# Last norm's second part: the spread of the factors by rounded single passes in place of native fp32 matmuls

## The chip, the cores and the metric

The kernel runs on one core of one Trainium2 chip. The metric is the device time of one execution in microseconds (us); the median of several executions counts. Engines run their own instruction streams and wait for each other by semaphores: TensorE (matmuls; PE in the rows, its weight loads PEld), VectorE (DVE), ScalarE (ACT), GpSimd (POOL) and SyncE (SP, which issues most DMAs here).

## What is computed

One layer of an encoder on x of 1024 tokens by 1024 channels: a SwiGLU block, a gated mixer, a cross-attention, a second SwiGLU block, and a last RMS norm. Only this last norm is touched:

```python
def _rms_norm(v, g):
    vf = v.astype(jnp.float32)
    r = lax.rsqrt(jnp.mean(vf * vf, axis=-1, keepdims=True) + EPS)
    return (vf * r).astype(v.dtype) * g

h = h + 0.5 * _swiglu(_rms_norm(h, ffn2_norm[l]), ffn2_w_gate[l], ffn2_w_up[l], ffn2_w_down[l])
return _rms_norm(h, final_norm)
```

## The kernel before

Activations lie transposed in SBUF: `h` has 8 tiles m of 128 channels (on the partitions) by 1024 tokens. Token columns are treated in two halves of 512, c = 0 and c = 1. Nearly all of the kernel is matmuls at line 550, each fp32 operand split in a high and a low half of the rounded type fp32r (`x_hi`, `x_lo`), three single-pass products for one of full precision. A matmul of native fp32 leaves two weight loads and two passes in the trace, one of fp32r leaves one of each.

The down projection of the second SwiGLU finishes the half c = 1 of `h` first, then the half c = 0. The last norm therefore comes in two parts, first for c = 1, beside the last matmuls, then for c = 0, when no other matmul is left. The steps of a part:

- ScalarE squares tiles of `h`, VectorE adds the squares into `acc`, and TensorE sums over the channels with one-column matmuls against `ones` (`last_sums`, lines 789 and 796). The sums come out as columns: 128 tokens on the partitions, one column for each of the 4 blocks of 128 tokens.
- VectorE forms the mean (`mean_square`, line 1943), ScalarE the square root (`root`), VectorE the reciprocal and one correction step (`factor_columns`, lines 1968 to 1978). The factors then stand in `norm[:, 2, 0:4]`.
- The factors must be spread: each of the 128 partitions needs the factor of every token along its row. This is `last_spread`. For c = 1 the factors are split in halves, `norm_hi` (a cast to fp32r) and the rest, each is multiplied with the identity into `diag_hi`, `diag_lo` (128x512), and `ones_r` times these gives the rows: two passes of 512 columns, beside other matmuls. For c = 0 the column of factors, broadcast along the free axis to 128x128, is the stationary operand and `ident` the moving one, native fp32, for 4 blocks of tokens into each of two PSUM banks (lines 803 to 807): first `last_bank(0, 1)`, which VectorE reads, then `last_bank(1, 0)`, which ScalarE copies to `f_g` for GpSimd. A semaphore `s_fsp` is raised after each bank. TensorE waits for `s_fac` at 4 before it.
- VectorE multiplies its tiles by the gain and the factor (`scale_last`, line 2479: six tiles for c = 0), and GpSimd two (tiles 5 and 7), which ScalarE has multiplied by the gain beforehand. SyncE stores each tile of VectorE's as it is done (line 1186), ScalarE's queue stores those of GpSimd (line 1395). Each store is 128 partitions by 512 columns, 256 KB, eight for each half.

The order of the end is written out by hand: VectorE scales tiles 1 to 3 of c = 1 around the mean of c = 0, adds the last sum (line 2462), waits for ScalarE's root, does `factor_columns(n, s_fac)` (line 2463), and goes to the six scalings. At the start of the kernel (from line 2023) VectorE casts `ones` to `ones_r`, and does four small operations, before it waits for TensorE.

Of the kernel before, what the change touches and what calls it, by code (L numbers as in the profile page):

```python
# [5 lines left out]
F32 = mybir.dt.float32  # L6
F32R = mybir.dt.float32r
ALU = mybir.AluOpType
# [3 lines left out]
P = 128  # L12
# [3 lines left out]
HALF = 512  # L16
# [227 lines left out]
def build(nc, a):  # L244
    ctx = ExitStack()
    with ctx:
        def sem(name):
            return ctx.enter_context(nc.semaphore(name))

        def tensors(where, specs):  # L250
            return [where.enter_context(nc.sbuf_tensor(n, s, d)) for n, s, d in specs]
# [4 lines left out]
        with ExitStack() as v:  # L256
            diag_hi, diag_lo = tensors(v, [("diag_hi", [P, L], F32R), ("diag_lo", [P, L], F32R)])
        sq, rn = tensors(ctx, [("sq", [P, L], F32), ("rn", [P, L], F32)])
        gains, ones, ident = tensors(ctx, [("gains", [P, 6, KT], F32), ("ones", [P, P], F32), ("ident", [P, P], F32)])
        ones_r, norm_hi, nidx, turn8 = tensors(ctx, [("ones_r", [P, P], F32R), ("norm_hi", [P, L // P], F32R),  # L260
                                                     ("nidx", [P, NC], F32), ("turn8", [P, COLS], F32)])
        pscale, m8, dskip, edge, eye = tensors(ctx, [
# [2 lines left out]
        stat, norm, mem_rows = tensors(ctx, [("stat", [P, 2, 4, 4], F32), ("norm", [P, 4, L // P], F32),  # L265
                                             ("mem_rows", [P, N_MEM // P], F32)])
# [59 lines left out]
        def scratch(name, shape, dt=F32):  # L326
# [26 lines left out]
        s_msq, s_total, s_fac, s_fsp, s_mg, s_mn, s_xn = (sem(n) for n in  # L353
            ("mem_squared", "squares_totalled", "norm_on_diagonals", "first_norm_spread", "mem_scaled", "mem_normed",
             "x_normed"))
# [92 lines left out]
        def ffn_bank(f, *use):  # L448
            r = BANK_AT[f][use] % 8
            pair = (finished["pairs", f] + f + r // 2) % 4  # L450
            return ps[pair if f else FIRST_PAIRS[pair]][:, r % 2]
# [68 lines left out]
        def key_bank(j):  # L520
            return (ps[3][:, 0], ps[3][:, 1], ps[2][:, 0], ps[2][:, 1])[j]

        def last_bank(c, k):

            return ffn_bank(1, "dn", 5, 2 * (1 - c) + k)
# [17 lines left out]
        def _(pe):  # L543
# [256 lines left out]
            def last_spread(c):  # L800
                pe.wait_ge(s_fac, 4 - c)
                if c == 0:
                    for bank in (last_bank(0, 1), last_bank(1, 0)):
                        for t in range(HALF // P):
                            ins = nc.tensor.matmul(bank[:, t * P:(t + 1) * P], norm[:, 2, t:t + 1].to_broadcast([P, P]),
                                                   ident[:], start=True, stop=True)
                        ins.then_inc(s_fsp, 1)
                    return
                nc.tensor.matmul(last_bank(c, 1), ones_r[:], diag_hi[:, 0:HALF], start=True, stop=False)
                nc.tensor.matmul(last_bank(c, 1), ones_r[:], diag_lo[:, 0:HALF], start=False, stop=True).then_inc(s_fsp, 1)  # L810
# [52 lines left out]
            for k in range(KT):  # L863
                w = kv_weights(k)
                pe.wait_ge(s_mg, k + 1)
                for t in range(2):
                    for c in range(2):
                        ins = nc.tensor.matmul(ps[t][:, c], mem_g[:, k, t * P:(t + 1) * P],  # L868
                                               w[:, c * HALF:(c + 1) * HALF], start=k == 0, stop=k == KT - 1)
# [17 lines left out]
            for m in range(KT):  # L887
# [5 lines left out]
                for k in range(KT):  # L893
                    ins = nc.tensor.matmul(key_bank(m // 2)[:, (m % 2) * N_MEM:(m % 2 + 1) * N_MEM], w[:, k],  # L894
                                           mem_n[:, k], start=k == 0, stop=k == KT - 1)
# [164 lines left out]
            ffn(1)  # L1060
            last_sums(0)
            last_spread(0)
            assert next(passes, None) is None

# [842 lines left out]
        def _(dve):  # L1907
# [3 lines left out]
            v = nc.vector  # L1911

            def link(ins, tally=step):

                tally.add()
                ins.then_inc(tally.sem, 1)
                dve.wait_ge(tally.sem, tally.at())

            def wait_act():
                dve.wait_ge(s_a2d, from_act.add())  # L1920
# [15 lines left out]
            def tt(out, x, y, op=ALU.mult, tally=step):  # L1936
                link(v.tensor_tensor(out, x, y, op), tally)  # L1937

            def ts(out, x, s1, s2=None, op0=ALU.mult, op1=None, tally=step):
                if op1 is None:  # L1940
                    link(v.tensor_scalar(out, x, s1, None, op0), tally)
                else:
                    link(v.tensor_scalar(out, x, s1, s2, op0, op1), tally)
# [4 lines left out]
            def cp(out, x, tally=step):  # L1948
                link(v.tensor_copy(out, x), tally)
# [18 lines left out]
            def factor_columns(n, signal=None, tally=step):  # L1968

                x, root, y, z = (norm[:, k, 0:n] for k in range(4))  # L1970
                wait_act()
                link(v.reciprocal(y, root))
                tt(z, y, y)
                tt(z, z, x)
                ts(z, z, -0.5, 1.5, ALU.mult, ALU.add)
                if signal:
                    v.tensor_tensor(y, y, z, ALU.mult).then_inc(signal, 1)
                else:
                    tt(y, y, z, tally=tally)
                return y, z  # L1980
# [41 lines left out]
                tt(mem_sq[:, 0:n], mem_sq[:, 0:n], mem_sq[:, n:2 * n], ALU.add, tally=totals if n == 1 else step)  # L2022
            dve.wait_ge(s_const, 16 * 2)
            cp(ones_r[:], ones[:])
            q = PL
            dve.wait_ge(s_pl, 16)
            tt(q["t4"], q["ar"], q["ar"])
# [13 lines left out]
            n = L // P  # L2041
# [4 lines left out]
            y, z = factor_columns(n, tally=to_act)  # L2046
# [161 lines left out]
            def ffn(f, gi, new=None, behind=lambda n: None, next_lo=None):  # L2208
# [167 lines left out]
                for n in range(f, FT):  # L2376
# [7 lines left out]
                    if f and n == 1:  # L2384
                        dve.wait_ge(s_spread, 1)
                        for c in range(2):
                            ins = v.tensor_copy(rn[:, c * HALF:(c + 1) * HALF], ffn_bank(f, "spread", c))
# [63 lines left out]
                if f == 0:  # L2451
                    next_low(f, KT - 1, KT - 2, next_lo, gi + 1)
                    for q in range(MP, KT):
                        add_next(f, q)
                else:
                    n = HALF // P
                    scale_last(1, 1)
                    scale_last(2, 1)
                    mean_square(last_bank(0, 0), n, step)
                    scale_last(3, 1)  # L2460
                    dve.wait_ge(s_norm, norms.add())
                    stt(norm[:, 0, 0:n], last_bank(1, 0)[:, 0:n], 1.0 / D, norm[:, 0, 0:n], ALU.mult, ALU.add, tally=to_act)
                    factor_columns(n, s_fac)
                    for m in range(KT):
                        if m not in POOL_FIRST:
                            scale_last(m, 0)
# [71 lines left out]
            def next_low(f, q, m, dst_lo, gi):  # L2538

                if m >= KT - 2:  # L2540
                    by, count = dn_op(f, DN_N - 2 if m == KT - 1 else DN_N - 3).low
                    dve.wait_ge(s_w_low[by], count)
                dve.wait_ge(s_bhi, q + 1)
                stt(dst_lo[:, m], h[:, m], gains[:, gi, m:m + 1], ua_hi[:, m].bitcast(F32), ALU.mult, ALU.subtract, tally=to_pe)
# [329 lines left out]
```

## Time and profile before

| | us |
|---|---|
| median of 3 runs | 2038.44 |
| lowest, highest | 2038.42, 2039.1 |
| the profiled execution | 2039.92 |
| its span, first to last instruction | 2038.1 |

| engine | busy us | share |
|---|---|---|
| TensorE | 2017.5 | 99% |
| VectorE | 1411.9 | 69% |
| GpSimd | 1199.4 | 59% |
| ScalarE | 654.5 | 32% |

The rows come from the one profiled execution. Times in them are us from the start of the span; PEclk is the clock that was granted to TensorE as a share of 2.4 GHz. A share of busy time is a mean over stages with different limits; here only the last 16 us and a few of the first are concerned, and they are read by timelines and by tables of short windows.

### The profile page before, as it was taken

What the parts mean: (1) busy time and instruction counts of PE and PEld (TensorE: products, weight loads), DVE (VectorE), ACT (ScalarE), POOL (GpSimd) and SP (SyncE); (2) the same over time, 40 slices, a digit from 0 to 9 for tenths busy, and PEclk for the clock granted to TensorE, in tenths of its full rate; (3) what the DMA queues carried; (4) which work ended last, traced back from release to release, by engine and by line L of the source; (5) the groups of instructions that cost most, each with busy time, mean ns of one, the idle gap of its engine ahead of it and who ended that gap; (6) DMA issues with size and microseconds to landing.
All of it is one profiled execution on the core that took longest, in us unless ns stands there. A gap on an engine that the chain in (4) does not pass through costs nothing.

```text
span 2038.1 us, 24606 instructions
## 1 busy us (share of the span) xinstructions
PE 2017.5 (99%) x9222; PEld 1657.4 (81%) x9222; DVE 1411.9 (69%) x1609; ACT 654.5 (32%) x1002; POOL 1199.4 (59%) x803
## 2 busy tenths in 40 slices
PE   9999999999999999999999999999999999999997
PEld 5888888888888888888888888787788888888886
DVE  7788768756976978663252455447876876789687
ACT  6423322333444501002131223235323233244443
POOL 6498888886545533223324321236899989865453
PEclk9999999999999999999999999999999999999999
DMA  7524333447976472432113331301233232288663
GB/s 272 177 79 152 105 138 104 144 161 283 311 236 218 128 189 69 124 95 56 52 50 126 106 122 45 122 32 62 79 134 98 85 128 99 88 295 289 221 211 135
DMA packets 141078, 286.39 MB, mean 141 GB/s; under 512 B 12832, under 2 KB 38048, under 8 KB 140576
## 3 DMA queue, kind: packets, MB, share of 16 engines
q1 hardware_dynamic: 100528, 232.68, 33.9%
q10 hardware_dynamic: 40432, 52.13, 8.0%
q8 instruction: 74, 1.21, 0.2%
q14 instruction: 44, 0.36, 0.1%
HBM read 222.39 MB, written 63.42 MB: 140 GB/s over the span
## 4 chain that ended last, share of the span: by engine, by line
PE 90%; DVE 6%; ACT 1%; issue 1%; POOL 1%; DMA 0%; POOLq 0%; SPq 0%; DVEq 0%; ACTq 0%
PE ps L550 86%; PE ps L894 1%; PE ps L868 1%; DVE w_lo L2527 1%; DVE h L2536 1%; DVE xt_lo L2517 1%; DVE ua_lo L1946 0%; DVE acc L1937 0%; POOL w_lo L1202 0%; DVE f_g L1937 0%; ACT xb_hi L1494 0%; DMA raw<-in_kv 0%; POOL h L1375 0%; POOL raw L1227 0%; ACT prob L1384 0%
## 5 line engine op out<-in xcount | busy, mean ns | idle before, releaser
L1202 POOL TENSOR_TENSOR w_lo<-raw,w_hi 128x512 fp32r<-128x512 f32 x352 | 543.2, 1556 | 197.4 <-ACT w_hi L1446 196.6
L550 PE MATMUL ps<-xt_hi,w_hi 128*128 128x512 f32 x1320 | 514.9, 390 | 2.7 <-DVE xt_lo L2517 1.4
L550 PE MATMUL ps<-xt_hi,w_lo 128*128 128x512 f32 x1320 | 513.6, 389 | 0.0
L550 PE MATMUL ps<-xt_lo,w_hi 128*128 128x512 f32 x1320 | 513.6, 389 | 0.0
L1446 ACT ACTIVATE w_hi<-raw 128x512 fp32r<-128x512 f32 x462 | 284.6, 625 | 460.7 <-PE ps L550 316.5
L1217 POOL TENSOR_SCALAR w_hi<-raw 128x1024 fp32r<-128x1024 f32 x53 | 62.4, 1178 | 456.5 <-PE ps L550 386.2
L550 PEld LDWEIGHTS ps<-xt_hi,w_hi 128*128 128x128 f32 x1320 | 247.7, 188 | 56.7 <-issue 2.5
L550 PEld LDWEIGHTS ps<-xt_hi,w_lo 128*128 128x128 f32 x1320 | 247.8, 188 | 51.8
L550 PEld LDWEIGHTS ps<-xt_lo,w_hi 128*128 128x128 f32 x1320 | 247.8, 188 | 50.9
L1227 POOL TENSOR_TENSOR raw<-raw 128x512 f32<-128x512 f32 x177 | 263.6, 1500 | 16.4 <-DMA raw<-in_gu 9.1
L550 PE MATMUL ps<-ua_hi,w_hi 128*128 128x512 f32 x608 | 237.4, 390 | 0.1
L550 PE MATMUL ps<-ua_lo,w_hi 128*128 128x512 f32 x608 | 236.6, 389 | 0.0
L1282 POOL TENSOR_TENSOR raw<-raw 128x512 f32<-128x512 f32 x110 | 164.7, 1502 | 121.1 <-DMA raw<-in_dn 120.7
L550 PE MATMUL ps<-xb_hi,w_hi 128*128 128x512 f32 x528 | 206.9, 392 | 2.2 <-POOL w_lo L1202 1.6
L550 PE MATMUL ps<-xb_lo,w_hi 128*128 128x512 f32 x528 | 205.6, 389 | 0.0
L550 PE MATMUL ps<-xb_hi,w_lo 128*128 128x512 f32 x528 | 205.5, 389 | 0.0
L550 PE MATMUL ps<-ua_hi,w_lo 128*128 128x512 f32 x608 | 187.3, 389 | 0.0
L1219 POOL TENSOR_TENSOR w_lo<-raw,w_hi 128x1024 fp32r<-128x1024 f32 x53 | 142.6, 2690 | 4.4
L2325 DVE TENSOR_TENSOR f_g<-ps,f_g 128x512 f32<-128x512 f32 x156 | 107.7, 690 | 45.1 <-ACT f_g L1548 21.0
L550 PEld LDWEIGHTS ps<-ua_hi,w_hi 128*128 128x128 f32 x608 | 114.1, 188 | 24.9 <-issue 0.9
L550 PEld LDWEIGHTS ps<-ua_hi,w_lo 128*128 128x128 f32 x608 | 114.1, 188 | 23.9
L550 PEld LDWEIGHTS ps<-ua_lo,w_hi 128*128 128x128 f32 x608 | 114.2, 188 | 23.5
(324 smaller groups left out, 2857.6 us busy)
## 6 DMA issues: line engine op xcount, KB each, us to landing
raw<-in_dn SPq DMA_DIRECT2D x264, 256.0 KB, 3.4
raw<-in_gu SPq DMA_DIRECT2D x88, 512.0 KB, 5.0
raw<-in_weights SPq DMA_DIRECT2D x54, 512.0 KB, 3.5
d_act<-f_g SPq DMA_DIRECT2D x20, 512.0 KB, 2.8
d_act<-acc SPq DMA_DIRECT2D x20, 512.0 KB, 2.8
d_act<-sq SPq DMA_DIRECT2D x20, 512.0 KB, 4.2
xt_hi<-d_act SPq DMA_DIRECT2D x20, 512.0 KB, 5.4
xt_lo<-d_act SPq DMA_DIRECT2D x20, 512.0 KB, 4.9
```

The costliest lines, as they stand in the source:

```text
L550: ins = nc.tensor.matmul(out, lhsT, rhs, start=start, stop=stop)
L868: ins = nc.tensor.matmul(ps[t][:, c], mem_g[:, k, t * P:(t + 1) * P], w[:, c * HALF:(c + 1) * HALF], start=k == 0, stop=k == KT - 1)
L894: ins = nc.tensor.matmul(key_bank(m // 2)[:, (m % 2) * N_MEM:(m % 2 + 1) * N_MEM], w[:, k], mem_n[:, k], start=k == 0, stop=k == KT - 1)
L1202: add(lo, src, hi.bitcast(F32), op=ALU.subtract).then_inc(s_w_low["pool"], 1)
L1217: nc.gpsimd.tensor_scalar(hi, src, 1.0, 0.0, ALU.mult, ALU.add).then_inc(s_w_hi, 1)
L1219: add(lo, src, hi.bitcast(F32), op=ALU.subtract).then_inc(s_w_low["pool"], 1)
L1227: add(out, x, y, op=op).then_inc(s_w_sum, 1)
L1282: add(raw_part(op, 0), raw_part(op, 0), raw_part(op, 1), op=ALU.add if w[2] > 0 else ALU.subtract).then_inc(s_w_sum, 1)
L1446: nc.scalar.activation(w_hi[:, op.halves[0]].rearrange("p k c -> p (k c)"), src, ACT.Copy).then_inc(s_w_high, 1)
L2325: link(v.tensor_tensor(out, x, y, ALU.add), adds)
L2517: v.tensor_tensor(xt_lo[:, 3, d % 4], acts_at(d // FP, d % FP), xt_hi[:, 3, d % 4].bitcast(F32), ALU.subtract).then_inc(s_a_lo, 1)
L2527: v.tensor_tensor(lo, raw_part(op, 0), hi.bitcast(F32), ALU.subtract).then_inc(s_w_low["dve"], 1)
```

## The change

For the half c = 0 the factors are now split in halves as well: `norm_hi` by a cast and a new tile `norm_lo` by a subtraction on VectorE, and the signal `s_fac` comes with the latter. `last_spread` makes two accumulating matmuls a block in place of one, with the broadcast column of `norm_hi` and then of `norm_lo` as the stationary operand and `ident_r`, a new fp32r copy of the identity, as the moving one. `ident_r` is cast once at the start, behind `ones_r`.

```diff
--- before.py
+++ after.py
@@ -257,6 +257,7 @@
             diag_hi, diag_lo = tensors(v, [("diag_hi", [P, L], F32R), ("diag_lo", [P, L], F32R)])
         sq, rn = tensors(ctx, [("sq", [P, L], F32), ("rn", [P, L], F32)])
         gains, ones, ident = tensors(ctx, [("gains", [P, 6, KT], F32), ("ones", [P, P], F32), ("ident", [P, P], F32)])
+        ident_r, norm_lo = tensors(ctx, [("ident_r", [P, P], F32R), ("norm_lo", [P, HALF // P], F32R)])
         ones_r, norm_hi, nidx, turn8 = tensors(ctx, [("ones_r", [P, P], F32R), ("norm_hi", [P, L // P], F32R),
                                                      ("nidx", [P, NC], F32), ("turn8", [P, COLS], F32)])
         pscale, m8, dskip, edge, eye = tensors(ctx, [
@@ -802,8 +803,9 @@
                 if c == 0:
                     for bank in (last_bank(0, 1), last_bank(1, 0)):
                         for t in range(HALF // P):
-                            ins = nc.tensor.matmul(bank[:, t * P:(t + 1) * P], norm[:, 2, t:t + 1].to_broadcast([P, P]),
-                                                   ident[:], start=True, stop=True)
+                            for part in (norm_hi, norm_lo):
+                                ins = nc.tensor.matmul(bank[:, t * P:(t + 1) * P], part[:, t:t + 1].to_broadcast([P, P]),
+                                                       ident_r[:], start=part is norm_hi, stop=part is norm_lo)
                         ins.then_inc(s_fsp, 1)
                     return
                 nc.tensor.matmul(last_bank(c, 1), ones_r[:], diag_hi[:, 0:HALF], start=True, stop=False)
@@ -2022,6 +2024,7 @@
                 tt(mem_sq[:, 0:n], mem_sq[:, 0:n], mem_sq[:, n:2 * n], ALU.add, tally=totals if n == 1 else step)
             dve.wait_ge(s_const, 16 * 2)
             cp(ones_r[:], ones[:])
+            cp(ident_r[:], ident[:])
             q = PL
             dve.wait_ge(s_pl, 16)
             tt(q["t4"], q["ar"], q["ar"])
@@ -2460,7 +2463,9 @@
                     scale_last(3, 1)
                     dve.wait_ge(s_norm, norms.add())
                     stt(norm[:, 0, 0:n], last_bank(1, 0)[:, 0:n], 1.0 / D, norm[:, 0, 0:n], ALU.mult, ALU.add, tally=to_act)
-                    factor_columns(n, s_fac)
+                    y, _ = factor_columns(n)
+                    cp(norm_hi[:, 0:n], y)
+                    v.tensor_tensor(norm_lo[:], y, norm_hi[:, 0:n].bitcast(F32), ALU.subtract).then_inc(s_fac, 1)
                     for m in range(KT):
                         if m not in POOL_FIRST:
                             scale_last(m, 0)
```

## Rows read from the trace of the kernel before

**Rows 1.** The page: busy us, share of the span and instructions of each engine.

```profile
PE 2017.5 (99%) x9222; PEld 1657.4 (81%) x9222; DVE 1411.9 (69%) x1609; ACT 654.5 (32%) x1002; POOL 1199.4 (59%) x803
```

**Rows 2.** Timeline of TensorE from 2022.9 us: start, length, instruction, releaser.

```profile
2023.14 0.95 PE L789 MATMUL ps<-ones,acc 128*128 128x1 f32 x8
2024.87 1.16 PE L796 MATMUL ps<-ones,sq 128*128 128x1 f32 x8 [0.79 <-ACT sq L1642]
2027.98 3.78 PE L805 MATMUL ps<-ident,norm 128*128 128x128 f32 x16 [1.94 <-DVE norm L1977]
```

**Rows 3.** Timeline of VectorE, the last six scalings.

```profile
2030.09 4.04 DVE L2479 SCALAR_TENSOR_TENSOR h<-h,gains,ps 128x512 f32<-128x512 f32 x6 [2.17 <-PE ps L805]
```

**Rows 4.** Timelines of ScalarE, GpSimd and ScalarE's queue, last 8 us.

```profile
2031.80 0.60 ACT L1626 ACTIVATE f_g<-ps 128x512 f32<-128x512 f32 x1 [5.04 <-PE ps L805]
2032.47 2.49 POOL L1375 TENSOR_TENSOR h<-h,f_g 128x512 f32<-128x512 f32 x2 [5.16 <-ACT f_g L1626]
2033.77 1.58 ACTq L1395 DMA_DIRECT2D out<-h  x2
```

**Rows 5.** Table of windows: busy time by engine, granted clock, DMA share, GB/s.

```profile
core 0: us, PE busy (x) PEld busy (x) DVE busy (x) ACT busy (x) POOL busy (x), PEclk, DMA share, GB/s
2025.00:2025.60 0.60, 0.60 (x7) 0.60 (x7) 0.60 (x2) 0.00 (x0) 0.60 (x1) 1.00 0.00 0
2025.75:2030.75 5.00, 3.06 (x15) 2.97 (x15) 2.36 (x8) 0.21 (x1) 1.56 (x2) 0.50 0.98 365
2030.75:2031.75 1.00, 1.00 (x5) 0.71 (x4) 1.00 (x3) 0.00 (x0) 0.00 (x0) 0.50 0.08 27
2031.75:2037.25 5.50, 0.01 (x1) 0.00 (x0) 2.38 (x4) 0.60 (x1) 2.49 (x2) 0.81 1.01 379
```

**Rows 6.** DMA issues from 2022 us: count, KB each, us from issue to landing.

```profile
out<-h SPq DMA_DIRECT2D x14, 256.0 KB, 2.1
out<-h ACTq DMA_DIRECT2D x2, 256.0 KB, 2.7
```

**Rows 7.** Timeline of VectorE in the norm's first part.

```profile
2015.84 0.17 DVE L1937 TENSOR_TENSOR norm<-norm 128x4 f32<-128x4 f32 x1
2016.04 0.17 DVE L1949 CAST norm_hi<-norm 128x4 fp32r<-128x4 f32 x1
...
2016.45 0.69 DVE L1937 TENSOR_TENSOR diag_hi<-ident,norm_hi 128x512 fp32r<-128x512 f32 x1
```

**Rows 8.** Timeline of TensorE in a narrow window (2028.6 to 2029) of the spread.

```profile
2028.35 1.06 PE L805 MATMUL ps<-ident,norm 128*128 128x128 f32 x4
```

**Rows 9.** Timeline of TensorE in the attention: rounded passes, then native ones.

```profile
1197.34 0.28 PE L550 MATMUL ps<-k_hi,ua_hi 128*128 128x256 f32 x1
1197.46 0.28 PE L550 MATMUL ps<-k_lo,ua_hi 128*128 128x256 f32 x1
...
1212.56 0.93 PE L1009 MATMUL ps<-ident,prob 128*128 128x128 f32 x7
```

**Rows 10.** Weight loads by line and shape: count, busy us, mean ns.

```profile
L550 PEld LDWEIGHTS ps<-xt_hi,w_hi 128*128 128x128 f32 x1320 | 247.7, 188 | 56.7 <-issue 2.5 <-DVE acc L2325 1.5 <-DVE xt_lo L2237 1.0
...
L550 PEld LDWEIGHTS ps<-u_t,e_m 128*64 128x64 f32 x128 | 6.9, 136 | 1.2 <-issue 0.4
...
L789 PEld LDWEIGHTS ps<-ones,acc 128*128 128x128 f32 x16 | 2.1, 191 | 0.2
...
L833 PEld LDWEIGHTS ps<-tables 128*32 128x32 f32 x64 | 1.5, 109 | 1.4 <-issue 0.7 <-DVE f_g L2325 0.7
```

**Rows 11.** Line 805: weight loads, ns min/median/max; then a narrow window with the first two.

```profile
L805 PEld LDWEIGHTS ps<-ident,norm x16: 285/333/333, 2028.0 to 2031.1; 128*128 128x128 f32 x16
...
2027.98 0.50 PEld L805 LDWEIGHTS ps<-ident,norm 128*128 128x128 f32 x2 [2.03 <-DVE norm L1977]
```

**Rows 12.** Timeline of VectorE at the start of the kernel.

```profile
11.09 0.23 DVE L1949 CAST ones_r<-ones 128x128 fp32r<-128x128 f32 x1
...
13.78 0.16 DVE L1943 TENSOR_SCALAR norm<-ps 128x2 f32<-128x2 f32 x1 [1.55 <-PE ps L851]
```

## The prediction

> **What bounds the kernel now.** Over the whole span it is TensorE, busy 99% [rows 1]. The change, though, touches only the last 10 us, so I read that stretch by itself: first the timeline of each engine, then the table by short windows, then the DMA issues. What TensorE does from 2022.9 us on [rows 2] is: eight one-column passes (the sums of squares), a wait, eight more, a wait of 1.94 us for VectorE's `norm`, and then the spread at line 805: 16 records in 3.78 us, with nothing else left beside them. Its 8 calls are native fp32, and each leaves two records of 128 columns. VectorE [rows 3] starts its six scalings at 2030.09, when the first bank (8 of the 16 records) is done; ScalarE starts the copy for GpSimd at 2031.80, when all 16 are [rows 4]. So the spread is on the path: nothing of it is hidden by TensorE's own work.
>
> Behind it comes a second limit. In the table of windows [rows 5] the DMA engines are full (0.98 at 365 GB/s) until 2030.75 with the stores of the half c = 1, then all but idle for the next 1.00 us (0.08), and full again (1.01 at 379 GB/s) for the 5.50 us to 2037.25. Eight stores of 256 KB [rows 6] are 2.10 MB, and at 379 GB/s these take 5.5 us: that is the whole of the last stretch. The end of the kernel is therefore the start of the first store of the half c = 0, plus 5.5 us of full DMA engines, plus 0.9 us to the end of the span. That first store follows VectorE's first scaling, so the **first bank** sets the end by this way; the **second bank** sets it another way (ScalarE's copy 0.60, two GpSimd products 2.49 to 2034.96, two stores issued from ScalarE's queue), and there the last store takes 2.7 us to land against 2.1 for one that finds the engines free [rows 4, 6]. So that way has 0.5 to 0.6 us to spare. And a gain has a ceiling: the idle time of the DMA engines is about 0.9 us (1.00 x 0.92), and stores that come earlier than that only queue behind those of the half c = 1.
>
> **The change part by part.** (1) VectorE: behind the last multiply of the factors it gains a cast to `norm_hi` and a subtraction to `norm_lo`, both 128x4, and the signal to TensorE moves behind the second. The same two operations stand in the first part of the same norm [rows 7]: multiply at 2015.84, cast at 2016.04, then the subtraction, and what follows it at 2016.45. So they cost 2016.45 - 2015.84 less the 0.20 of the multiply alone: **+0.41 us**, in full on the path, since TensorE waits for exactly this. Queued behind them on VectorE are only the six scalings, which wait for TensorE anyway. TensorE's first load moves from 2027.98 to about 2028.39.
>
> (2) TensorE: 8 calls of two records become 16 calls of one record, so 16 weight loads and 16 passes of 128 columns stay 16 and 16. What can shrink is the time of one. Before, records follow at 213 ns: the rows of narrow windows give 1.06 us for 4 of 421 ns each, (1.06 - 0.42) / 3 [rows 8]. That is 256 cycles at 1.2 GHz for 128 columns, two cycles for each; the granted clock there is 0.50 of 2.4 GHz, where it was 1.00 up to 2025.6, and fell after the one-column passes and the wait between them [rows 5]. A pass of the rounded type (fp32r) needs one cycle for a column: passes of 256 columns follow at 0.12 us at the full clock (1197.34, 1197.46), as long as native fp32 takes for half the columns there ((0.93 - 0.27) / 6 = 0.11 for 128) [rows 9]. If only the streaming counted, a 128-column pass would now cost 107 ns.
>
> But every pass has its own weight load, and the load doesn't get cheaper. Its cost is seen where nothing is streamed: the eight one-column passes at the full clock take 0.95 us [rows 2], the last of them 250 ns long, so (0.95 - 0.25) / 7 = 0.10 us apiece. The recorded load times give the same in another way: 109 ns for 32 columns, 136 for 64, 191 for 128 [rows 10], 0.85 ns a column, two cycles of 2.4 GHz, so about 107 ns for 128. And fp32r loads are no shorter than native ones: 188 ns for `w_hi` against 191 for native `ones` [rows 10]. At the clock of the spread the load record is 333 ns instead of 191 [rows 10, 11], longer by 142; a doubled 107 accounts for 107 of it, and a doubled 53 would account for 53. So I take the load as 256 cycles: 213 ns at 1.2 GHz, just what the native pass took. Loads run ahead under passes, so the spacing is the longer of the two: max(213, 107) = 213 ns, and the stream of 16 is as long as before. Two corrections remain. The last pass of each bank streams 107 ns less behind its load: -0.1 us. The fp32r passes show some 12 ns on top of their streaming (0.12 against 0.107) [rows 9]: +0.1 us for 8, +0.2 for 16. Together **-0.1 to +0.1 us**, taken as 0.
>
> (3) `cp(ident_r, ident)`, a cast of 128x128, at the start. The same cast of `ones` took 0.23 us [rows 12]. Soon behind it VectorE waits 1.55 us for TensorE's first sums: hidden, 0 us; were that cover gone it would cost 0.26. The spread needs its result 2 ms later. (4) Two more tensors (512 and 16 bytes a partition) move what is allocated behind them. No row prices that; the repeats of one program lie within 0.7 us, and I take 0, with 0.3 either way.
>
> **Sum**, against the profiled execution (span 2038.1, its own time 2039.92): +0.41 + 0 + 0 = +0.4. First bank 0.4 later, first store 0.4 later, the DMA engines full for the same 5.5 us; second bank 0.4 later and inside its spare 0.5 or with it. Span 2038.5. The median of the runs, 2038.44, is 1.5 below the profiled one; from it, **2038.8 us**, and 2038.4 to 2039.3 with the bounds above. If the clock were high during the spread, both kinds would follow at about 0.11 us [rows 2, 9] and the sum would be the same.
>
> **Rivals.** *Cheap passes* (faster): the fp32r load takes one cycle a column after all, or overlaps better, and passes follow at 107 ns. First bank: 7 intervals shorter by 106 and the last pass by 107, -0.85, with the 0.41 a net -0.4: the DMA stream starts 0.4 earlier and the time is 2038.0. The second bank gains 15 x 0.106 + 0.1 - 0.41 = 1.3, of which nothing arrives, since its stores find the engines full. It breaks even at a spacing of 213 - (0.41 - 0.11)/7 = 170 ns. With a clock that is high as well it goes to the ceiling of 0.9: 2037.5. For it speaks the unexplained rest of the load record (142 against 107) and that the second load of the spread starts only 0.17 us after the first (0.50 - 0.333) [rows 11]; against it the slope of the load times. 0.16. [...]
>
> *Dear short passes* (slower): an fp32r pass narrower than 256 columns doesn't reach one cycle a column but four, or is split. The narrowest fp32r passes of the trace are those of 256 columns [rows 9], so nothing excludes it. Then 427 ns each at 1.2 GHz. First bank: 7 x 0.214 + 0.21 + 0.41 = +2.1; the stream of stores starts 2.1 later: 2040.6. If the clock stays low to the end of it, the second bank decides: 15 x 0.214 + 0.21 + 0.41 = +3.8, less the 0.6 that its way has to spare: 2041.6. It decides from 213 ns upwards for every ns; 0.2% of the time (4.1 us, about what a measurement of this kernel can tell from no change) would need some 490 ns a pass. Against it speaks only that 256 columns show no penalty. 0.17.
>
> *Something in the placement or the rest* that moves the 2000 us before, either way: 0.05.
>
> **How the numbers follow.** Forecast as likeliest 0.62: 2038.8. To hold 8 in 10 the range must take in most of both rivals: 2037.6 to 2041.6. No case but the last reaches 0.2% (2034.4 or 2042.5): faster 0.01, same 0.96, slower 0.03.
>
> **What would show it.** After: line 805's records single, 16 or so, at 213 ns and each about 314 ns long instead of 421; the first one at about 0.4 us further from `norm`; VectorE's scalings and ScalarE's copy both 0.3 to 0.5 later against the last sums; the DMA gap 0.4 longer and the full stretch again 5.5 us. A spacing near 107 ns at clock 0.50 proves the first rival and the load term wrong, one near 427 the second. Stores of the half c = 0 that do not start with VectorE's first scaling would prove the DMA part wrong.

## The result

| | before | after |
|---|---|---|
| median of the runs, us | 2038.44 | 2087.65 |
| lowest, highest | 2038.42, 2039.1 | 2087.34, 2087.87 |
| the profiled execution, its span | 2039.92, 2038.1 | 2087.54, 2085.7 |

The changed kernel takes 1.0239 times as long, 95% interval 1.0227 to 1.0252: 49 us more, where 2038.8 us was predicted. Those 49 us cannot lie in the last norm: the part of it that the change touches lasted 10 us before. The page of after shows the engines as before [rows 1], with the same 9222 passes, and 50 us more of busy TensorE; then the chain of waits, and three groups of the costliest ones (busy us, mean ns of one, idle before):

```profile
span 2085.7 us, 24609 instructions
PE 2067.2 (99%) x9222; PEld 1655.3 (79%) x9222; DVE 1396.9 (67%) x1612; ACT 655.2 (31%) x1002; POOL 1184.1 (57%) x803
...
PE 94%; DVE 2%; ACT 1%; DMA 1%; POOL 1%; issue 1%; POOLq 0%; SPq 0%; DVEq 0%; ACTq 0%
...
L551 PE MATMUL ps<-xt_hi,w_hi 128*128 128x512 f32 x1320 | 522.1, 396 | 0.9 <-POOL w_lo L1204 0.5
L551 PE MATMUL ps<-xt_lo,w_hi 128*128 128x512 f32 x1320 | 521.4, 395 | 0.0
```

The same two views of before, the chain and one of the groups:

```profile
PE 90%; DVE 6%; ACT 1%; issue 1%; POOL 1%; DMA 0%; POOLq 0%; SPq 0%; DVEq 0%; ACTq 0%
...
L550 PE MATMUL ps<-xt_hi,w_hi 128*128 128x512 f32 x1320 | 514.9, 390 | 2.7 <-DVE xt_lo L2517 1.4
```

TensorE was the bound and is it still more: its share of the chain went from 90% to 94%, VectorE's fell from 6% to 2%. And line 551, the old line 550, which the change does not touch, has longer records: 396 ns against 390. Records of passes overlap, so the price of one pass is read from starts. TensorE in the middle of the kernel, before, three starts of the same step:

```profile
639.64 0.39 PE L550 MATMUL ps<-xt_hi,w_hi 128*128 128x512 f32 x1
...
640.32 0.39 PE L550 MATMUL ps<-xt_hi,w_hi 128*128 128x512 f32 x1
...
641.00 0.39 PE L550 MATMUL ps<-xt_hi,w_hi 128*128 128x512 f32 x1
```

and after:

```profile
640.04 0.39 PE L551 MATMUL ps<-xt_hi,w_hi 128*128 128x512 f32 x1
640.27 0.40 PE L551 MATMUL ps<-xt_lo,w_hi 128*128 128x512 f32 x1
640.50 0.39 PE L551 MATMUL ps<-xt_hi,w_lo 128*128 128x512 f32 x1
640.74 0.40 PE L551 MATMUL ps<-xt_hi,w_hi 128*128 128x512 f32 x1
```

A step of three passes took 0.68 us and takes 0.70. As a mean over the 1250 or so unbroken steps of `xt` in a trace it is 680.2 ns before and 700.1 after, 226.7 and 233.4 a pass. A window of 34 us in which TensorE is never idle counts the same thing (passes that overlap its ends are counted in): first before, then after. The granted clock is 1.00 in both, so this is no clock.

```profile
core 0: us, PE busy (x) PEld busy (x) DVE busy (x) ACT busy (x) POOL busy (x), PEclk, DMA share, GB/s
640.00:674.00 34.00, 34.00 (x152) 28.15 (x151) 27.80 (x37) 17.30 (x29) 19.88 (x13) 1.00 0.59 184
```

```profile
640.00:674.00 34.00, 34.00 (x147) 27.30 (x146) 24.95 (x35) 13.96 (x24) 20.32 (x15) 1.00 0.65 211
```

The kernel makes 8136 such passes, three-pass products with a weight of `w_hi` or `w_lo` and 512 columns streamed: 3 x 1320 of `xt`, 3 x 608 of `ua`, 3 x 528 of `xb`, 3 x 128 of `ub`, and 192 each of `mixed` and `y`. The mean start-to-start (of starts less than 300 ns apart) of every one of these six kinds rose from between 226.7 and 227.1 to 233.2 or 233.3 ns. 8136 x 6.5 ns = 53 us, of which 49 reach the end. Some 2 us of the rest went into waits that TensorE had before (its idle time fell from 20.6 to 18.5 us): with slower passes VectorE is late less often, which is its fall in the chain. The other 2 are not placed: the product counts every pass as part of an unbroken stream, and not all are.

Nor is it traffic of the other engines. Among the `xt`, `ua` and `xb` passes there are 372 after during which VectorE, ScalarE and GpSimd were idle and no DMA packet was under way: their mean is 233.3 ns. The 326 such passes before have 226.8.

What the change does to these passes is only to move one of their operands. In SBUF `w_hi` and `w_lo` are allocated ahead of `ident_r` and `norm_lo`, the streamed operands behind. In the program built from the kernel before, `w_hi` starts at byte 16512 of a partition and `xt_hi` at 130176; in that of after, at 16512 and at 130720, 544 bytes later. Of the 544, `ident_r` has 512, from 62784, and `norm_lo` 32 for its 16, from 63296 to `ones_r` at 63328. The runs count in the same way: the change with 32, 96 or 224 more unused bytes goes like the kernel before with a plain pad of 64, 128 or 256 (steps of 686.7, 700.0 and 680.2 ns, both times), so its own tensors count as 544, and not as 528.

### The profile page after: what moved, and what is told of

The parts are those of the page before. It is cut to its first block, busy times and chain, and to the rows that moved or that the text cites. A ratio compares the mean times of both kernels' runs of the same rounds, so it can differ in the third digit from the quotient of the medians.

```text
span 2085.7 us, 24609 instructions
## 1 busy us (share of the span) xinstructions
PE 2067.2 (99%) x9222; PEld 1655.3 (79%) x9222; DVE 1396.9 (67%) x1612; ACT 655.2 (31%) x1002; POOL 1184.1 (57%) x803
## 4 chain that ended last, share of the span: by engine, by line
PE 94%; DVE 2%; ACT 1%; DMA 1%; POOL 1%; issue 1%; POOLq 0%; SPq 0%; DVEq 0%; ACTq 0%
PE ps L551 91%; PE ps L896 1%; DMA raw<-in_kv 1%; PE ps L870 1%; POOL w_lo L1204 0%; DVE f_g L1939 0%; ACT xb_hi L1496 0%; POOL h L1377 0%; POOL raw L1229 0%; ACT prob L1386 0%; DVE ua_lo L1939 0%; ACT ua_hi L1386 0%; DVE stat L2737 0%; DVE pt_lo L1939 0%; PE ps L823 0%
## 5 line engine op out<-in xcount | busy, mean ns | idle before, releaser
L1204 POOL TENSOR_TENSOR w_lo<-raw,w_hi 128x512 fp32r<-128x512 f32 x352 | 531.5, 1520 | 236.5 <-ACT w_hi L1448 235.2
L551 PE MATMUL ps<-xt_hi,w_hi 128*128 128x512 f32 x1320 | 522.1, 396 | 0.9 <-POOL w_lo L1204 0.5
L551 PE MATMUL ps<-xt_lo,w_hi 128*128 128x512 f32 x1320 | 521.4, 395 | 0.0
L551 PE MATMUL ps<-xt_hi,w_lo 128*128 128x512 f32 x1320 | 521.4, 395 | 0.0
L551 PE MATMUL ps<-ua_lo,w_hi 128*128 128x512 f32 x608 | 240.9, 396 | 0.0
```

What stands on the lines that cost most here:

```text
L551: ins = nc.tensor.matmul(out, lhsT, rhs, start=start, stop=stop)
L1204: add(lo, src, hi.bitcast(F32), op=ALU.subtract).then_inc(s_w_low["pool"], 1)
```

## The experiments

Two numbers are given for each run: the median with its ratio to before on the same chip, and the **step**, the mean of a step of three `xt` passes in its trace. "Distance" is by how many bytes the start of the streamed operands was moved against that of the weights, against before; there all these starts lie multiples of 1024 bytes apart. The expectations name the rule that I held when each was written: first the placement against the instructions of the change, then a start that must be a multiple of 64 bytes, then a distance by 128, and at last one by 256. Ratios in brackets are 95% intervals.

### Is it the change or the place?

The kernel before with two tensors that nobody uses, of the size of the new ones:

```diff
+        tensors(ctx, [("pad_a", [P, 128], F32)])
+        tensors(ctx, [("pad_b", [P, 4], F32)])
```

> The kernel before with nothing changed but two unused tensors of 512 and 16 bytes a partition, allocated where the change puts ident_r and norm_lo (544 bytes with the rounding to 32). In the changed kernel all passes of 512 columns with w_hi or w_lo as weights follow at 233.3 ns instead of 226.7. Theory A (placement: what is allocated behind the two tensors starts 32 bytes past a multiple of 64 instead of on one, and the passes read slower there): 2087.3, as the changed kernel, with 233.3 ns. Theory B (the new instructions do it, in whatever way): 2038.4 with 226.7 ns.

2087.72 us, ratio 1.024 (1.0226 to 1.0254), step 700.1 ns: the whole loss, without one instruction of the change. Its passes:

```profile
640.00 0.39 PE L552 MATMUL ps<-xt_lo,w_hi 128*128 128x512 f32 x1
640.23 0.40 PE L552 MATMUL ps<-xt_hi,w_lo 128*128 128x512 f32 x1
640.47 0.39 PE L552 MATMUL ps<-xt_hi,w_hi 128*128 128x512 f32 x1
640.70 0.40 PE L552 MATMUL ps<-xt_lo,w_hi 128*128 128x512 f32 x1
```

The change with its two tensors allocated behind `h`, so that no operand of the long products moves:

```diff
         gains, ones, ident = tensors(...)
-        ident_r, norm_lo = tensors(...)
...
         h = ...
+        ident_r, norm_lo = tensors(...)
```

> The change with all its instructions, but ident_r and norm_lo are allocated last, behind h, so that every other tensor starts where it did before. Theory A: 2038.6 to 2038.9, the change's own price (VectorE's two operations +0.41, the spread of 16 passes shorter by about 0.1 to 0.2), with 226.7 ns a pass. Theory B: 2087.

2039.63 us, ratio 1.0003 (0.9994 to 1.0012), step 680.2. The loss is gone, all instructions of the change are there. Its window, with the count of before:

```profile
640.00:674.00 34.00, 34.00 (x152) 28.15 (x151) 28.28 (x37) 16.04 (x27) 20.03 (x13) 1.00 0.59 187
```

These two settle where the 49 us come from. The next ones ask what in the placement counts.

### An operand's own start, or the distance between two?

The change, and one pad of 32 bytes behind it (576 in all, so every start is a multiple of 64 again):

```diff
         ident_r, norm_lo = ...
+        tensors(ctx, [("pad", [P, 8], F32)])
```

> The change as it is, with 32 more unused bytes behind norm_lo, so that the tensors behind it are moved by 576 bytes and start on a multiple of 64, but not of 128 as before. Theory A with a step of 64 bytes: 2038.6 to 2038.9, as with the tensors allocated last. With a step of 128 bytes: 2087. Theory B: 2087.

2055.03 us, ratio 1.008 (1.0067 to 1.0094), step 686.7: neither cured nor as bad, a third level. In the window:

```profile
640.00:674.00 34.00, 34.00 (x150) 27.87 (x150) 28.38 (x37) 15.91 (x26) 19.01 (x14) 1.00 0.61 192
```

The kernel before with 32 bytes ahead of `w_hi`, so that weights and streamed operands all start at odd multiples of 32, and keep their distance:

```diff
+        tensors(ctx, [("pad", [P, 8], F32)])
         w_hi, w_lo, raw = tensors(...)
```

> The kernel before with 32 unused bytes ahead of w_hi: weights and moving operands alike start 32 bytes past a multiple of 64. Theory A1 (the moving operand's own start decides): 2087, 233.3 ns. Theory A2 (what decides is how the weights' start stands to the moving operand's; in the changed kernel the weights stayed and the rest moved by 32 modulo 64, while the passes over pw_hi and mixed, pooled tensors that moved together with their weights kept 226.7 to 227.4 ns): 2038.4, 226.7 ns.

2039.15 us, ratio 1.0002 (0.9993 to 1.0011), step 680.2: no loss. That an operand starts at an odd multiple of 32 does not matter by itself. The counterpart moves the weights by 32 and the rest by 64:

```diff
+        tensors(ctx, [("pad", [P, 8], F32)])
-        w_hi, w_lo, raw = tensors(...)
+        w_hi, w_lo, _, raw = tensors(... ("pad2", [P, 8], F32), ("raw", ...))
```

> The kernel before with w_hi and w_lo moved by 32 bytes and everything behind them by 64, so that only the distance between weights and moving operands is 32 modulo 64, while the moving operands start on a multiple of 64. Moving all by 32 left 226.8 ns a pass; moving only the rest by 544 gave 233.3, by 576 about 229 (2055 us). Theory A2 (the distance between the weights' start and the moving operand's counts): 2087, 233.3 ns. If the moving operand's own start counted after all, and e5's 2039 had another cause: 2038 or 2055, 227 or 229 ns.

2087.96 us, ratio 1.0242 (1.0212 to 1.0272), step 700.0. The streamed operands start where a plain pad of 64 bytes puts them (step 686.7, below), the weights stand 32 further, and the price is another. `raw` and the other tensors up to `ident` stand elsewhere as well, 64 further than with the plain pad. But here they keep their distance to the streamed operands, and in the first pad experiment they kept theirs to the weights, with the full loss both times. What changed in both is the distance of the weights and the streamed operands, here to 32.

### Which distances?

96 bytes, in the kernel before:

```diff
         gains, ones, ident = ...
+        tensors(ctx, [("pad", [P, 24], F32)])
```

> The kernel before with 96 unused bytes where the change puts its tensors: the distance is 96 modulo 128. So far: 0 gives 226.7 ns, 64 gives 226 to 232 (mean 229), 32 gives 233.3. Theory A2 with a period of 128 bytes and the cost growing with the distance to the nearest multiple of 128: 96 is as 32, 2087. Theory A3, any distance of 32 modulo 64 is dear: also 2087. If the direction counts (96 is 32 ahead of the next multiple): another value, between 2038 and 2120.

2088.3 us, ratio 1.0244 (1.0214 to 1.0274), step 700.0.

128 bytes, as the change with 96 more (640 in all):

```diff
         ident_r, norm_lo = ...
+        tensors(ctx, [("pad", [P, 24], F32)])
```

> The change as it is, with 96 more unused bytes behind norm_lo, so that the tensors behind it are moved by 640 bytes, five times 128. Moves by 32, 96 and 544 gave 2088, by 576 2055. If the start modulo 128 is all that counts: 2038.6 to 2039.5 and 226.7 ns, the change's own 0.3 us on top of the kernel before. If a larger period counts (256 or more): above 2050.

2083.32 us, ratio 1.0215 (1.0198 to 1.0232), step 700.0. A rule by 128 bytes falls with it: the window has the count of after, not that of before.

```profile
640.00:674.00 34.00, 34.00 (x147) 27.39 (x146) 24.13 (x33) 14.12 (x25) 20.09 (x14) 1.00 0.69 221
```

Then one plain pad each, in the same place of the kernel before, of 16, 32, 64 and 128 words:

```diff
         gains, ones, ident = ...
+        tensors(ctx, [("pad", [P, N], F32)])
```

> The kernel before with 64 unused bytes where the change puts its tensors. 576 gave 687 ns a step and 2055. Period of 512 bytes (theory S512): the same, 687 and 2055. Period of 1024 or more (S1024): another value, most likely 700 and 2088 as for most distances.

> 128 unused bytes. 640 gave 700 ns and 2083. S512: 700. S1024: open. With w_hi at a distance of 128 and w_lo at 96 or 64 it was 700 too.

> 256 unused bytes. Period of 256: 680 ns and 2038.5. S512 or S1024: 687 to 700, 2055 to 2088. Below 680 would be a placement better than the present one.

> 512 unused bytes, which is also the change with norm_lo elsewhere: ident_r alone moves the rest by just this. S512: 680 ns and 2038.5. S1024: 687 to 700, 2055 to 2088.

And 192 bytes, 48 words:

> The kernel before with 192 unused bytes. If the distance counts by its size to the nearest multiple of 256, as 64: 687 ns a step and 2055. If the direction counts: another value, 700 and 2083 to 2088 being the most frequent so far.

| pad, bytes | median, us | ratio | step, ns |
|---|---|---|---|
| 64 | 2054.75 | 1.0079 (1.005 to 1.0108) | 686.7 |
| 128 | 2083.69 | 1.0221 (1.0192 to 1.0251) | 700.0 |
| 192 | 2088.0 | 1.024 (1.0221 to 1.0259) | 700.0 |
| 256 | 2038.82 | 0.9999 (0.9988 to 1.0011) | 680.2 |
| 512 | 2039.26 | 1.0 (0.9988 to 1.0011) | 680.2 |

256 and 512 bytes are free, everything tried between is not. 64 equals 576, 128 equals 640 (to 0.4 us each) and 32 equals 544 (700 ns where only the weights moved by 32 and the rest by 64, and 700 after), so the price repeats with 256 or 512 bytes; since 256 itself is free, 256 is the simplest reading. 192 is not the mirror of 64: the distance has a sign. With 128 bytes the kernel is some 4 us quicker than with 32, 96 or 192 at the same `xt` step; half of it is in the other kinds, `ua`, `ub`, `mixed` and `y`, which go at 232.4 ns instead of 233.3 there (2592 passes x 0.9 = 2.3 us). The other 2 us I did not place.

### Parts of a step

A step reads two weights and two streamed halves. In the kernel before, only `xt_lo` and `ub_lo` are moved by 32 (`ub_lo` in the same way as shown, with one more pad behind `x_sq` in the memory that `x_sq`, `xt` and `ub` share), `xt_hi` keeps its distance. What is allocated behind `ub_lo` moves by 32 too, `y` and the attention's `k` among it:

```diff
-            xt_hi, xt_lo = tensors(...)
+            xt_hi, _, xt_lo = tensors(... ("pad_xt", [P, 8], F32), ...)
```

> The kernel before with only the low halves xt_lo and ub_lo moved by 32 bytes (and the mixer's and attention's small tensors behind them). Each in three passes streams from them. w_lo alone moved by 32 made all three passes of a step slower (230 + 236 + 234 = 700 ns in place of 680), as much as everything moved. Theory P (each pass pays for its own operands): a third of the price where xt_lo is used, 687 ns a step, about 2050. Theory S (one operand out of step disturbs the whole rhythm of three passes): 700 ns a step wherever xt_lo or ub_lo is used, 693 or less for xb and ua, about 2075.

2058.95 us, ratio 1.0097 (1.0077 to 1.0118). The `xt` step is 695.2 ns (231.7, 233.0, 230.5), that of `xb`, which is not moved, 680.8. By kinds this adds up: 3960 x 5.0 ns of `xt`, 384 x 3.1 of `ub` and 192 x 6.7 of `y`, which was moved as well, are 22 us, measured 20 against the 2038.86 of before there. But one pass in three reads the moved half, and all three are slower: the price isn't only that of a pass whose two own operands stand badly.

This run is also the only one in which the distance of the two operands of a 256-column pass changes: `k` moved by 32 bytes, `ua`, its weights, did not. In all the other kernels these passes follow at 119.5 to 119.8 ns, here at 116.8: a distance of 32 makes them quicker. Three starts of the same kind, three passes apart: 0.35 us, where it was 0.36 before.

```profile
1208.94 0.28 PE L550 MATMUL ps<-k_hi,ua_hi 128*128 128x256 f32 x1
...
1209.29 0.28 PE L550 MATMUL ps<-k_hi,ua_hi 128*128 128x256 f32 x1
...
1209.64 0.28 PE L550 MATMUL ps<-k_hi,ua_hi 128*128 128x256 f32 x1
```

The weights one by one. `w_lo` alone by 32, everything behind by 128; `w_lo` alone by 64, everything behind by 128 (16 and 16 words); and both weights starting 16 bytes into a larger tensor, everything behind by 128 (distance 112):

```diff
-        w_hi, w_lo, raw = tensors(...)
+        w_hi, _, w_lo, _, raw = tensors(... ("pad_a", [P, 8], F32), ... ("pad_b", [P, 24], F32), ...)
```

```diff
+        both, raw = tensors(ctx, [("w_both", [P, 2 * RING * KP * P + 32], F32R), ("raw", [P, 2, D], F32)])
+        w_hi, w_lo = (both[:, 4 + k * RING * KP * P:...].rearrange(...) for k in range(2))
```

> The kernel before with w_lo alone moved by 32 bytes (everything behind it by 128). Per step of the contraction there are three passes: w_hi with the high half of x, w_hi with the low half, w_lo with the high half. Theory P (a pass is slowed by the distance between its own weights and its own moving operand): only the third pass is slow, 233 ns, 2038 + 49 / 3 = 2055. Theory N (a pass is slowed when the weights of the next pass, loaded while it streams, stand 32 off its moving operand): only the second is slow, also 2055. If the distance between w_hi and w_lo counted too, more than 2055.

> The kernel before with w_lo alone moved by 64 bytes (everything behind it by 128). With x as a whole moved by 64 a step of three passes took 687 ns and the kernel 2055. Theory S (any operand out of step, and the distance sets how much): 687 ns a step, 2055. Theory P: a third of it, 682, 2044.

> The kernel before with w_hi and w_lo started 16 bytes into a larger tensor, everything behind moved by 128. The distance between weights and moving operands is then 16 bytes modulo 32. If what counts is the distance modulo 128 at any grain: 2088 or more. If only blocks of 32 bytes count: weights that straddle two blocks at their ends, 2038 to 2045. A value under 2038 would show that the even placement isn't the best one.

2088.5 us (1.0245, 1.0215 to 1.0275), 2083.75 (1.0219, 1.0199 to 1.024) and 2082.3 (1.0212, 1.0192 to 1.0232); steps 700.0 ns for the first two, and 233.3 a pass of `xt` in the third. They were built when I took 128 bytes for harmless, so that the pad behind would undo the move for all but the weight in question. It was not harmless, and the three say no more than that distances of 64 to 128, mixed, cost a step what 128 alone costs; in the total the last two are like 128, the first, with its 96, like 96. Within a step the passes do shift: 230.3, 236.1, 233.6 ns in the first, where `w_lo` stands 96 off, and 235.9, 231.0, 233.1 in the second, with 64.

### What the change itself costs

The kernel with the change and a pad that brings the distance to 768, a multiple of 256:

```diff
         ident_r, norm_lo = ...
+        tensors(ctx, [("pad", [P, 56], F32)])
```

> The change as it is, with 224 more unused bytes behind norm_lo: the tensors behind it are moved by 768 bytes, three times 256. With a period of 256: 680 ns a step, 2038.9 to 2039.5, the 0.3 us of the change's own tail on top. If the 0.3 us is real the stretch from the last sums of squares to the end is 13.46 to 13.56 us, against 13.24 before.

2038.94 us, ratio 1.0000 (0.9991 to 1.0009), window as before:

```profile
640.00:674.00 34.00, 34.00 (x152) 28.16 (x151) 28.01 (x37) 17.30 (x29) 17.73 (x13) 1.00 0.60 189
```

To see the spread's own price and what sets the end, the version with its tensors behind `h` was cut to its high half: one cast, 8 passes. This leaves out the low half of the factors.

```diff
-                            for part in (norm_hi, norm_lo):
+                            for part in (norm_hi,):
...
-                    cp(norm_hi[:, 0:n], y)
-                    v.tensor_tensor(norm_lo[:], y, norm_hi[:, 0:n].bitcast(F32), ALU.subtract).then_inc(s_fac, 1)
+                    v.tensor_copy(norm_hi[:, 0:n], y).then_inc(s_fac, 1)
```

> The change with its tensors allocated last, with the high half of the factors alone: one cast on VectorE, no subtraction, 8 passes in place of 16; it leaves the low half of the factors out. It prices the tail. The weight load bounds the passes at 213 ns (seen: 415 ns records 213 apart at the clock of 0.50), so the first bank is ready 4 x 213 + 200 = 1.05 us sooner than with both halves, the second 8 x 213 + 200 = 1.9 sooner. If the stores bound the end by their 5.5 us of full DMA engines and by what is still queued of the half c = 1: span about 0.6 to 0.9 below that of the kernel before (2037.3 to 2037.5 on the scale of 2038.1), and the idle time between the two groups of stores nearly gone. If GpSimd's way (second bank) set the end: 1.5 below. In the median it will be lost in the spread of the runs, 1 us either way.

2037.93 us, ratio 0.9997 (0.9985 to 1.0008): not told apart from before by its time, but by its timeline. Of TensorE, VectorE and GpSimd in its last part:

```profile
2023.85 1.05 PE L797 MATMUL ps<-ones,sq 128*128 128x1 f32 x8 [0.78 <-ACT sq L1644]
...
2027.19 1.97 PE L807 MATMUL ps<-ident_r,norm_hi 128*128 128x128 f32 x8 [2.28 <-DVE norm_hi L2467]
2028.34 4.04 DVE L2483 SCALAR_TENSOR_TENSOR h<-h,gains,ps 128x512 f32<-128x512 f32 x6 [1.21 <-PE ps L807]
...
2029.87 2.50 POOL L1377 TENSOR_TENSOR h<-h,f_g 128x512 f32<-128x512 f32 x2 [3.55 <-ACT f_g L1628]
```

and its table of windows around the gap of the DMA engines:

```profile
2024.75:2029.75 5.00, 2.12 (x10) 1.85 (x9) 3.28 (x11) 0.76 (x2) 1.56 (x2) 0.59 0.97 365
2029.75:2030.00 0.25, 0.00 (x0) 0.00 (x0) 0.25 (x1) 0.04 (x1) 0.13 (x1) 0.50 0.28 99
2030.00:2035.50 5.50, 0.00 (x0) 0.00 (x0) 2.38 (x4) 0.00 (x0) 2.36 (x2) 0.50 1.01 377
```

To compare tails, times are counted from the start of the second eight one-column passes (2024.87 in [rows 2]):

| us from there to | spread starts | VectorE's first scaling | end of span |
|---|---|---|---|
| before | 3.11 | 5.22 | 13.24 |
| before, 32 bytes ahead of `w_hi` | 3.11 | 5.22 | 13.24 |
| before, 256 bytes of pad | 3.12 | 5.23 | 13.26 |
| before, 544 bytes of pad | 3.04 | 5.15 | 13.17 |
| after | 3.42 | 5.43 | 13.46 |
| change, tensors behind `h` | 3.53 | 5.54 | 13.56 |
| change, distance 768 | 3.51 | 5.52 | 13.55 |
| change, tensors behind `h`, high half only | 3.34 | 4.49 | 12.54 |

## Why the prediction was wrong

**The step that failed is (4)**, the two more tensors: "No row prices that; the repeats of one program lie within 0.7 us, and I take 0, with 0.3 either way." Measured: +49 us for the 544 bytes, by the kernel that has the pad and not the change. The bound was drawn from the wrong thing. Repeats of one program all have the same placement, and cannot tell what another one does; nothing in the trace excluded either a loss or a gain, and the term stood against 8136 passes on the bound engine, so that 1 ns a pass is 8 us. The third rival, placement, was named and given 0.05, without a price and without its place among the operands. What could have been seen before: TensorE's operands stand on both sides of the new tensors, all at multiples of 1024 bytes from each other, and the change ends that. That this has a price, and which, no row of before could show.

The other steps, with placement held (change with tensors behind `h`, against before):

(1) **VectorE's cast and subtraction, +0.41.** Spread start 3.53 against 3.11: +0.42. Right; the fourteen kernels without the change lie between 3.02 and 3.16 there, so this is good to about 0.1. In the changed kernel itself:

```profile
2075.06 0.16 DVE L1939 TENSOR_TENSOR norm<-norm 128x4 f32<-128x4 f32 x1
2075.26 0.17 DVE L1951 CAST norm_hi<-norm 128x4 fp32r<-128x4 f32 x1
2075.47 0.16 DVE L2468 TENSOR_TENSOR norm_lo<-norm,norm_hi 128x4 fp32r<-128x4 f32 x1
```

(2) **Sixteen passes as long as before, the last of a bank 0.1 shorter.** They follow at 213 ns at the low clock, as the native ones did [rows 8]: right. So is the load of 213 ns that this rests on. Where only one column is streamed behind each load, the sums' passes follow at 112 ns at the full clock, and at 215 and 213 ns in the version with its tensors behind `h`, whose clock fell to 0.50 in the middle of them. From the spread's start to VectorE's first scaling it is 2.01 us against 2.11, the 0.1 of the forecast, but not for its reason: that is luck. VectorE starts 0.46 us after the start of the bank's last pass before, and 0.45 after. What got shorter is the first gap: the second pass starts 0.37 us behind the first before (2028.35 - 2027.98 [rows 2, 8]) and 0.27 after. Why is open. After, in narrow windows, the first two of the spread and two of its middle:

```profile
2075.68 0.47 PE L807 MATMUL ps<-ident_r,norm_hi 128*128 128x128 f32 x1 [2.37 <-DVE norm_lo L2468]
2075.95 0.41 PE L807 MATMUL ps<-ident_r,norm_lo 128*128 128x128 f32 x1
...
2077.66 0.41 PE L807 MATMUL ps<-ident_r,norm_lo 128*128 128x128 f32 x1
2077.88 0.41 PE L807 MATMUL ps<-ident_r,norm_hi 128*128 128x128 f32 x1
```

Wrong was what the records would show: 415 ns each, not 314. The length of a record did not shrink with the streaming time that I took for it. Both rivals of this step are out: cheap passes would follow at 107 ns, dear ones at 427. The cycles that this step counts in, at 2.4 GHz for a clock of 1.00 and 1.2 GHz for 0.50, are an estimate that the traces bear out: from 256 to 512 columns the spacing of fp32r passes in the kernel before rises from 119.6 to 226.7 ns at a clock of 1.00, 0.418 ns a column, which is 2.39 GHz at one column a cycle; 256 columns of native fp32 take 215.8 ns there, 0.843 a column, and 128 take 213 ns at 0.50, 1.67 a column.

(3) **`ident_r` hidden.** No run has it alone. The wait that was to cover it is not always there: it was 1.55 us in the profiled execution of before, whose clock was 0.50 from 8.4 to 11.8 us, and it is gone after, where the clock stayed at 1.00, and in the kernels with unused pads of 256 and 544 bytes, which have no cast. After, TensorE's first sums ended at 11.93 us and VectorE came to them only at 12.47. With distance 768 or the tensors behind `h` nothing is left of it that a ratio of 1.0000 or 1.0003 could show.

**The end.** From VectorE's first scaling to the end it is 8.02 to 8.05 us in all eight rows of the table. In the version with the high half alone the first bank came 0.73 earlier than before and the second 1.6 (GpSimd starts at 2029.87, 6.02 after the one-column passes, against 2032.47 - 2024.87 = 7.60 [rows 2, 4]), and the end moved by 0.70, as the first bank did. So the stores set the end and the second bank's way has room, as was said; and the gap of the DMA engines has shrunk from 0.9 us to about 0.2 (0.25 at 0.28), which is the ceiling seen from close by. After, the full stretch is the same, as forecast, and the gap is longer, by less than the 0.4 of the forecast: no packet was under way for 0.78 us before, for 0.99 after and for 1.10 with the tensors behind `h`:

```profile
2073.25:2078.25 5.00, 2.63 (x13) 2.57 (x13) 2.39 (x10) 0.20 (x1) 1.36 (x2) 0.63 0.98 364
2078.25:2079.25 1.00, 1.00 (x6) 0.92 (x5) 1.00 (x3) 0.00 (x0) 0.00 (x0) 0.50 0.00 0
2079.25:2084.75 5.50, 0.11 (x1) 0.00 (x0) 2.48 (x4) 0.60 (x1) 2.49 (x2) 0.50 1.02 378
```

So the sum of the change's own terms was +0.4, and +0.3 is what its tail shows (13.56 or 13.55 against 13.24, and 13.46 after against 13.17 with the same placement and no change); a -0.1 is there, at the first gap, and the +0.1 against it is not. That is below what the medians can tell: with placement held the change makes no measurable difference. No version tried is faster than before; the pads that are free give its step of 680.2 ns, and none gives less.

**What stays open** is how the distance acts inside. Shown is, for the passes with 512 columns: it is the distance of stationary and streamed operand, not an address; 0, 256, 512 and 768 bytes are free (680.2 ns a step); one badly placed operand slows the passes beside it as well (231.7, 233.0 and 230.5 ns with `xt_lo` 32 bytes off). Passes of 256 columns follow another rule, of which there is one value (116.8 ns at 32 bytes); that `k_hi`, `ua_hi` still go at 0.12 us after says nothing, as both stand behind the new tensors and moved together. The native fp32 passes of 256 columns do not react: those of `mem_n` with weights of `raw` take 215.8 ns in every kernel, also where the one moved and the other did not.

Loads run beside streaming, PEld is busy 83% of the window of before, so a collision of the load's reads with those of the streaming is my guess. It is argued, not shown: no run took the loads away or moved them in time. The kept traces speak for it at one place and leave it open at others. After, six passes of `mx_pooled` with `pw` as weights, all behind the new tensors, stand between passes with `w_lo` and `w_hi`:

```profile
780.19 0.62 PE L551 MATMUL ps<-ua_hi,w_lo 128*128 128x512 f32 x2
780.65 1.07 PE L551 MATMUL ps<-mx_pooled,pw_hi 128*128 128x512 f32 x4
781.55 0.62 PE L551 MATMUL ps<-mx_pooled,pw_lo 128*128 128x512 f32 x2
782.01 0.39 PE L551 MATMUL ps<-ua_hi,w_hi 128*128 128x512 f32 x1
```

From start to start these are 230 and 227 ns, then 227, 226, 227, 227, 226 and 235, here and at the next two such places, and within 1 ns the same with the pad of 544 alone. The last pass with `w_lo`, whose own operands stand badly, is quick, and the last with `pw_lo`, whose own stand well, is slow: as if what counts were the weights that are loaded meanwhile, those of the next pass. But where `pt` and `v`, both moved, follow on `ub`, the last pass of `ub` takes 233 ns, and seven of the next (236, 224, 231, 236, 228, 233, 230 or 231) go by before it is 227. Such uneven passes stand in the kernel before as well, wherever a row of them begins after a break (235, 229, 232, 231, then 227 at the last group of `mx_pooled`). So a disturbance lasts for several passes, which may be why one badly placed operand in three makes all three slower.

## What to carry to other kernels

A new tensor is not free because it is small: on a kernel bound by TensorE, look at which operands stand ahead of it and which behind, and allocate it last, or fill it up to a multiple of 256 bytes a partition (shown here for passes of 512 columns in fp32r, 226.7 ns against 229 to 233.3; those of 256 columns were quicker 32 bytes off, 116.8 ns against 119.6). When a change is timed, time the kernel before with an unused tensor of the same size beside it; here that would have told a harmless edit (1.0003) from its placement (1.024). And the spread of repeats is no bound for a term that every repeat holds fixed.

## What the runs showed of the hardware

Passes of fp32r with 512 columns, each with its own weight load, follow at 226.7 ns when stationary and streamed operand start a multiple of 256 bytes apart within a partition (0, 256, 512 and 768 beyond multiples of 1024 were run), at 229 ns with 64 bytes more, and at 233.3 ns with 32, 96, 128 or 192 more (some kinds at 232.4 with 128). In the changed kernel, 544 bytes off, which is 32 more than 512, this is worth 49 us of 2038.
